# A convolution's last sums moved between engines, a weight slot passed over one group later, and loads that wait

## The chip, the cores and the metric

One core of one Trainium2 chip runs the whole program. The metric is the device time of one execution in microseconds (us), as the median over runs. The engines are TensorE (PE), VectorE (DVE), ScalarE (ACT), GpSimd (POOL) and SyncE (SP, which here issues transfers only).

## The reference, cut to what matters

Two layers over 256 tokens of width 2048, all in float32. Layer 0 mixes tokens by a convolution module, layer 1 by latent attention; each is followed by a SwiGLU block with a hidden width of 5632.

```python
def conv_module(h, w_pw1, b_pw1, w_dw, b_dw, ln_g, ln_b, w_pw2, b_pw2):
    a, gate = jnp.split(h @ w_pw1 + b_pw1, 2, axis=-1)
    v = a * jax.nn.sigmoid(gate)
    v = depthwise causal convolution of v over the tokens, 31 taps per channel, + b_dw
    v = jax.nn.silu(layernorm(v, ln_g, ln_b))
    return v @ w_pw2 + b_pw2

h = h + conv_module(rmsnorm(h), ...)                    # layer 0; layer 1: h + mla(rmsnorm(h), ...)
h = h + (silu(r @ w_gate) * (r @ w_up)) @ w_down        # r = rmsnorm(h), in both layers
```

## The kernel before, in words

**Split weights.** A float32 product is made as three faster products of "high" and "low" parts. So each weight group (1 MB, 128 x 2048 numbers, usually 4 blocks of 128 rows by 512 columns) is loaded into a slot of `raw`; ScalarE copies it, rounded, to `w_hi` (`hi`, `f_hi`), then VectorE writes the rest `raw - w_hi` to `w_lo` (`lo`, `f_lo`), and TensorE multiplies. `raw`, `w_hi` and `w_lo` have four slots each. SyncE waits until the low part of a slot's last group is made before it loads the next group there; ScalarE waits until TensorE has used the slot of `w_hi` and `w_lo`.

**The convolution.** The first product (`w_pw1`) is made in eight halves, s = 0 to 7, each of two tiles (mm = 0, 1) of 128 channels by 256 tokens, from four groups j = 0 to 3. For j = 2 and 3 the low part is not made by VectorE: ScalarE writes the negative high part to `w_lo`, and GpSimd issues a transfer that adds `raw` to it (`conv_low`, semaphore `lo_added`). After TensorE has the tiles, ScalarE makes the sigmoid of the gate (`gate_sigmoid`), VectorE multiplies (`gated`), and the 31 taps are shared out. For s < 7 ScalarE makes 10 products of a tap with the shifted tile into slots of `row_bc`, GpSimd adds them up for both tiles at once (128 x 512, `conv_sums`), and VectorE does the other 21 taps in PSUM (`tap`, a multiply-add each) and adds GpSimd's sum to them. In the last half TensorE does 12 of the taps with diagonal matrices (`conv_rows_last`, which ends with a product for the finished sums, after the wait for `conv_step`); ScalarE does 5 and VectorE 14. Then come the statistics of the layer norm (`row_stats`), the norm, the transposes and the second product (`w_pw2`, groups from G_PW2 on). In the last half TensorE makes tile 0 first (`last_tile0`). ScalarE copies the high part of the first `w_pw2` group between the two tiles.

**The SwiGLU block** (`ffn(l)`, l = 0, 1) goes through the hidden width in 11 chunks of 512, c = 0 to 10. For c >= 1 the parts of one chunk run in the order Q1, R1, Q3, Q5, D0, R2, D1, Q6, D2, Q7, Q2 and so on; Q, R, G and U are groups of the gate and up weights (the Q and R ones form block products by Strassen's method), D0 to D3 are groups of the down weights that use the hidden values of chunk c - 1. TensorE's own order is Q1, R1, Q3, the transposes of chunk c - 1 (`hidden`), Q5, D0, R2, D1, Q6, D2. After the transposes ScalarE writes `a_hi` and VectorE `a_lo`, both in their functions `hidden(c - 1)`; D0 needs both. R2's weights are sums of others: VectorE's `t1_lo_and_t2` and `t2_lo_and_t4` and ScalarE's `t1_hi` and `t2_hi` make them in turn. The slot of a group in `w_hi` and `w_lo` goes round by position (`f_w`); since 182 groups in a layer are not a multiple of four, two slots are passed over, in the chunks 3 and 6 (`F_SKIPS`), at D0. Each engine has one queue in program order, written out by hand in the four blocks.

Of the kernel before, what the change touches and what calls it, by code (L numbers as in the profile page):

```python
# [36 lines left out]
S = 256  # L37
# [7 lines left out]
RING = 4  # L45
# [9 lines left out]
DIAG_PART = 2 * PE_TAPS_LAST // (HALVES - 2)  # L55

PROD_TAPS = (10,) * (HALVES - 1) + (5,)
PROD_TAP = [sum(PROD_TAPS[:s]) for s in range(HALVES + 1)]
PROD_ADD = [sum(PROD_TAPS[:s]) - s for s in range(HALVES + 1)]
# [83 lines left out]
def f_w(q):  # L143


    return (q + sum(q >= f_pos(c, D0) for c in F_SKIPS)) % RING
# [28 lines left out]
def prod_tap0(s):  # L175
    return PE_TAPS_LAST if s == HALVES - 1 else 0


def dve_tap0(s):
    return prod_tap0(s) + PROD_TAPS[s]  # L180

DVE_STEP = [1 + 2 * sum(TAPS - dve_tap0(r) + 1 for r in range(s)) for s in range(HALVES + 1)]
# [23 lines left out]
def encoder(nc, x, positions, attn_norm_g, ffn_norm_g, final_norm_g, conv_w_pw1, conv_b_pw1, conv_w_dw,  # L208
# [3 lines left out]
    with ctx:  # L212
# [279 lines left out]

        def norm_counts(n):

            return KT * n
# [18 lines left out]
        def _(sp):  # L514
# [40 lines left out]
            def square_loads(w, g0):  # L555
                for j in range(KG):
                    load(tile_rows(w, slice(GK * j, GK * j + GK), slice(0, CH)), g0 + j)
                with sp.Fori(0, CC - 1) as i:
                    for j in range(KG):
                        load(tile_rows(w, slice(GK * j, GK * j + GK), bass.ds(i * CH + CH, CH)), g0 + KG + j, i, KG)  # L560
            for n in range(CC):
# [3 lines left out]
            def ffn_loads(l):  # L565
                wg, wu, wd = ffn_w_gate[l], ffn_w_up[l], ffn_w_down[l]

                def f_load(q, src):
# [5 lines left out]
                    elif l == 0:  # L574
                        sp.wait_ge(out_added, TT)
                        sp.wait_ge(prod_added, PROD_ADD[HALVES])
# [80 lines left out]
        def _(pool):  # L657
# [15 lines left out]
            def conv_sums(s):  # L673
# [3 lines left out]
                for n in range(1, PROD_TAPS[s]):  # L677
                    pool.wait_ge(prod_done, 2 * (PROD_TAP[s] + n) + 2 if s < HALVES - 1 else
                                 2 * PROD_TAP[s] + PROD_TAPS[s] + n + 1)
# [5 lines left out]
            for s in range(HALVES):  # L685
# [3 lines left out]
                conv_sums(s)  # L689
# [14 lines left out]
            pool.wait_ge(prod_added, PROD_ADD[HALVES])  # L704
# [26 lines left out]
        def _(act):  # L731
# [75 lines left out]
            def product_of(s, n, mm):  # L807

                m, tile, w = 2 * (s % 2) + mm, 2 * s + mm, prod_tap0(s) + n
                if n == 0 and s >= 2:  # L810
                    act.wait_ge(conv_tr, TT * (s - 1))
                elif n > 0 and PROD_ADD[s] + n > PROD_SLOTS:
# [4 lines left out]
                dst = acc[:, m, :] if n == 0 else prod_slot(s, n)[:, S * mm:S * mm + S]  # L817
# [32 lines left out]
            for mm in range(2):  # L850
                gate_sigmoid(HALVES - 1, mm)
                for n in range(PROD_TAPS[HALVES - 1]):
                    product_of(HALVES - 1, n, mm)
# [55 lines left out]
            def ffn(l):  # L909
# [87 lines left out]
                for c in range(1, FC):  # L997
                    parts_hi(c, D0)
                    t1_hi(c)
                    q1_out(c)  # L1000
                    hidden(c - 1)
                    t2_hi(c)
# [140 lines left out]
        def _(dve):  # L1143
# [109 lines left out]
            def conv_half(s):  # L1253
# [3 lines left out]
                w0 = dve_tap0(s)  # L1257
                steps = TAPS - w0
# [9 lines left out]
                def tap(w, mm):  # L1268
                    m, tile = 2 * u + mm, 2 * s + mm
                    if w == w0:  # L1270
# [5 lines left out]
                    dve.wait_ge(conv_step, DVE_STEP[s] + (steps * mm + w - w0 if last else 2 * (w - w0) + mm - 1))  # L1276
                    dve.scalar_tensor_tensor(bank[mm], vbuf[:, m, w:w + S], tap_col[:, w, tile:tile + 1],
                                             bank[mm], ALU.mult, ALU.add).then_inc(conv_step, 1)

                if last:  # L1280
                    for mm in range(2):
                        gated(mm)
                        for w in range(w0, TAPS):
                            tap(w, mm)
                else:
                    gated(0)
                    gated(1)
                    lo(G_PW1 + KG * (s + 1) + 1)
                    for w in range(w0, TAPS):
                        tap(w, 0)  # L1290
                        tap(w, 1)
                    if s < HALVES - 2:
                        lo(G_PW1 + KG * (s + 2))
                for mm in range(2):
                    m = 2 * u + mm
                    dve.wait_ge(prod_added, PROD_ADD[s + 1])
                    dve.wait_ge(conv_step, DVE_STEP[s] + (steps * (mm + 1) if last else 2 * steps + mm - 1))
                    dve.tensor_tensor(acc[:, m, :], acc[:, m, :], bank[mm], ALU.add).then_inc(conv_step, 1)
# [140 lines left out]
            def ffn(l):  # L1439
# [137 lines left out]
                for c in range(1, FC):  # L1577
                    parts_lo(c, D0)
                    t1_lo_and_t2(c)
                    hidden(c - 1)  # L1580
# [748 lines left out]
```

## Time and profile before

| | us |
|---|---|
| median of 3 runs (2004.69 to 2005.74) | 2005.21 |
| the profiled execution: its own time | 2006.77 |
| the profiled execution: span from first to last instruction | 2004.9 |
| PE busy | 1957.0 |
| DVE busy | 1623.5 |
| ACT busy | 1144.8 |
| POOL busy | 223.3 |

The span is what the trace covers; the 1.9 us between it and the execution's own time lie outside of the records. Matmuls are pipelined, so two that follow each other overlap in the records: what counts is the distance from start to start.

### The profile page before, as it was taken

To read this page: it belongs to the slowest core of one execution; us is meant where nothing else is said; L and a number is where in the kernel's file an instruction comes from. 1 tells how busy PE (TensorE), PEld (TensorE's weight loads), DVE (VectorE), ACT (ScalarE), POOL (GpSimd) and SP (SyncE) were. 2 spreads that over 40 slices of the span, in tenths; PEclk is the share of its full clock that TensorE was granted. 3 is DMA by queue.
4 is the path that set the end of the run, shared out by engine and by line. 5 is a ranking of instruction groups with operands and counts; after the bars stand their busy time and mean duration, and the time that the engine had idled before them with its cause. 6 is when DMAs were issued, how large, how long until landed. Compare 5 with 4: busy or idle time off the path is not lost.

```text
span 2004.9 us, 25061 instructions
## 1 busy us (share of the span) xinstructions
PE 1957.0 (98%) x9934; PEld 1669.9 (83%) x9934; DVE 1623.5 (81%) x1782; ACT 1144.8 (57%) x1140; POOL 223.3 (11%) x187
## 2 busy tenths in 40 slices
PE   8999799999999999999999999999999999999998
PEld 7999788888788888888888998887888888888886
DVE  7999896888888888888876774588888888888885
ACT  5888644555555555555544654356555555655553
POOL 0555200010010100100010000000110000100002
PEclk9999899999999999999999999999999999999999
DMA  8999364899999989999845435559989999999983
GB/s 277 254 254 259 114 213 152 235 266 276 237 227 258 263 273 244 226 264 253 249 155 141 136 135 177 191 176 276 242 225 256 262 278 232 231 257 264 279 210 126
DMA packets 253830, 453.37 MB, mean 226 GB/s; under 512 B 18708, under 2 KB 60444, under 8 KB 251420
## 3 DMA queue, kind: packets, MB, share of 16 engines
q1 hardware_dynamic: 207968, 349.73, 50.3%
q0 software_dynamic: 44256, 98.57, 28.6%
q10 hardware_dynamic: 1500, 3.61, 0.5%
q8 instruction: 72, 1.18, 0.2%
q14 instruction: 34, 0.28, 0.0%
HBM read 435.10 MB, written 2.10 MB: 218 GB/s over the span
## 4 chain that ended last, share of the span: by engine, by line
PE 81%; DMA 9%; DVE 6%; ACT 2%; issue 2%; SPq 0%; POOL 0%; ACTq 0%; DVEq 0%; POOLq 0%
PE ps L1769 77%; DMA raw<-in_conv_w_pw_dram 4%; DMA w_lo<-raw 3%; DVE w_lo L1159 2%; DMA raw<-in_ffn_w_up_dram 1%; PE ps L2010 1%; ACT w_lo L751 1%; ACT w_hi L896 1%; PE ps L2264 0%; PE ps L2265 0%; PE ps L2245 0%; DMA resid<-in_x_dram 0%; DVE raw L1527 0%; DVE w_lo L1525 0%; DVE x_lo L1186 0%
## 5 line engine op out<-in xcount | busy, mean ns | idle before, releaser
L1159 DVE TENSOR_TENSOR w_lo<-raw,w_hi 128x2048 fp32r<-128x2048 f32 x224 | 510.2, 2291 | 148.6 <-ACT w_hi L896 148.6
L896 ACT ACTIVATE w_hi<-raw 128x2048 fp32r<-128x2048 f32 x224 | 426.9, 1916 | 347.4 <-PE ps L1769 215.6
L1769 PE MATMUL ps<-w_hi,x_hi 128*128 128x512 f32 x1168 | 455.7, 390 | 2.2 <-DVE x_lo L1344 1.4
L1769 PE MATMUL ps<-w_hi,x_lo 128*128 128x512 f32 x1168 | 454.5, 389 | 0.0
L1769 PE MATMUL ps<-w_lo,x_hi 128*128 128x512 f32 x1168 | 454.4, 389 | 0.0
L1769 PE MATMUL ps<-w_hi,a_hi 128*128 128x512 f32 (+1 forms) x768 | 292.9, 381 | 7.4 <-DVE a_lo L1444 7.4
L1769 PE MATMUL ps<-w_hi,a_lo 128*128 128x512 f32 (+1 forms) x768 | 292.1, 380 | 0.0
L1769 PE MATMUL ps<-w_lo,a_hi 128*128 128x512 f32 (+1 forms) x768 | 292.0, 380 | 0.0
L1769 PEld LDWEIGHTS ps<-w_hi,x_hi 128*128 128x128 f32 x1168 | 219.3, 188 | 49.1 <-DVE x_lo L1186 1.4
L1769 PEld LDWEIGHTS ps<-w_hi,x_lo 128*128 128x128 f32 x1168 | 219.2, 188 | 45.8
L1769 PEld LDWEIGHTS ps<-w_lo,x_hi 128*128 128x128 f32 x1168 | 219.3, 188 | 45.2
L746 ACT ACTIVATE w_hi<-raw 128x2048 fp32r<-128x2048 f32 x88 | 167.0, 1913 | 94.3 <-PE ps L1769 69.8
L696 POOL DMA_DIRECT2D raw<-in_ffn_w_up_dram x60 | 77.1, 1285 | 1245.2 <-DVE w_lo L1159 1245.2
L1154 DVE TENSOR_TENSOR w_lo<-raw,w_hi 128x2048 fp32r<-128x2048 f32 x74 | 169.0, 2290 | 41.0 <-ACT w_hi L746 40.7
L1769 PEld LDWEIGHTS ps<-w_hi,a_hi 128*128 128x128 f32 x768 | 144.4, 188 | 36.8 <-issue 9.7
L1769 PEld LDWEIGHTS ps<-w_hi,a_lo 128*128 128x128 f32 x768 | 144.5, 188 | 27.6
L1769 PEld LDWEIGHTS ps<-w_lo,a_hi 128*128 128x128 f32 x768 | 144.5, 188 | 27.1
L1159 DVE TENSOR_TENSOR w_lo<-row_bc,w_hi 128x2048 fp32r<-128x2048 f32 x60 | 137.4, 2290 | 31.8 <-ACT w_hi L896 31.7
L1769 PE MATMUL ps<-x_hi,w_hi 128*128 128x256 f32 (+1 forms) x512 | 147.4, 288 | 11.0 <-DMA w_lo<-raw 11.0
L896 ACT ACTIVATE w_hi<-row_bc 128x2048 fp32r<-128x2048 f32 x60 | 114.6, 1911 | 58.1 <-PE ps L1769 58.1
L1769 PE MATMUL ps<-x_lo,w_hi 128*128 128x256 f32 (+1 forms) x512 | 145.7, 284 | 0.0
L1769 PE MATMUL ps<-x_hi,w_lo 128*128 128x256 f32 (+1 forms) x512 | 145.7, 284 | 0.0
(241 smaller groups left out, 2996.0 us busy)
## 6 DMA issues: line engine op xcount, KB each, us to landing
raw<-in_ffn_w_down_dram SPq DMA_DIRECT2D x66, 1024.0 KB, 8.1
raw<-in_ffn_w_up_dram POOLq DMA_DIRECT2D x60, 1024.0 KB, 8.8
raw<-in_ffn_w_gate_dram SPq DMA_DIRECT2D x50, 1024.0 KB, 6.3
raw<-in_ffn_w_up_dram SPq DMA_DIRECT2D x48, 1024.0 KB, 5.9
row_bc<-in_ffn_w_gate_dram SPq DMA_DIRECT2D x38, 1024.0 KB, 5.6
raw<-in_conv_w_pw_dram SPq DMA_DIRECT2D x64, 512.0 KB
row_bc<-in_ffn_w_down_dram SPq DMA_DIRECT2D x22, 1024.0 KB, 5.8
b<-in_ffn_w_up_dram SPq DMA_DIRECT2D x40, 512.0 KB, 5.1
```

The costliest lines, as they stand in the source:

```text
L696: pool.dma_start(f_raw_tile(l, q).rearrange("p (k n) -> p k n", k=GK), w_of(l, p, c), accum_op=ALU.add).then_inc(f_added[f_raw(q)], 16)
L746: act.activation(w_hi[:, slot, :], raw[:, slot, :], ACT.Copy).then_inc(hi_done, 1)
L751: act.activation(w_lo[:, slot, :], raw[:, slot, :], ACT.Copy, scale=-1.0).then_inc(neg_done, 1)
L896: act.activation(f_w_tile(w_hi, l, q), f_raw_tile(l, q), ACT.Copy).then_inc(f_hi_done, 1)
L1154: dve.tensor_tensor(w_lo[:, g % RING, :], raw[:, g % RING, :], hi32(w_hi[:, g % RING, :]), ALU.subtract).then_inc(lo_dve, 1)
L1159: dve.tensor_tensor(f_w_tile(w_lo, l, q), f_raw_tile(l, q), hi32(f_w_tile(w_hi, l, q)), ALU.subtract).then_inc(f_lo_done, 1)
L1769: ins = pe.matmul(dst, lhsT, rhs, start=first and n == 0, stop=last and n == len(pairs) - 1, skip_group_check=skip)
L2010: ins = pe.transpose(ps[:, hidden_bank(c) + b, S * kk + P * t:S * kk + P * t + P], ff_h[:, t, P * m:P * m + P], ident[:, :])
```

## The change

The last half of the convolution is shared out anew: ScalarE makes 8 products for tile 0 and 7 for tile 1 (5 and 5 before), VectorE does 11 and 12 taps (14 and 14), TensorE 12 as before. GpSimd adds these products up tile by tile, in instructions of 128 x 256 (7 and 6; before 4 of 128 x 512 for both), from eight small slots, and VectorE adds GpSimd's sum to its own right behind the taps of each tile. SyncE waits for GpSimd's two adding transfers of the last half before it loads the first `w_pw2` groups. The slot passed over in the chunks 3 and 6 is passed over at D1, not at D0. In chunk 1 `a_lo` is made ahead of the sums for R2, on VectorE and on ScalarE.

```diff
 DIAG_PART = 2 * PE_TAPS_LAST // (HALVES - 2)
-PROD_TAPS = (10,) * (HALVES - 1) + (5,)
-PROD_TAP = [sum(PROD_TAPS[:s]) for s in range(HALVES + 1)]
-PROD_ADD = [sum(PROD_TAPS[:s]) - s for s in range(HALVES + 1)]
+PROD_LAST = (8, 7)
+PROD_TAPS = (10,) * (HALVES - 1)
+PROD_TAP = [sum(PROD_TAPS[:s]) for s in range(HALVES)]
+PROD_ADD = [sum(PROD_TAPS[:s]) - s for s in range(HALVES)]
+PROD_ADD_LAST = [PROD_ADD[HALVES - 1] + sum(PROD_LAST[:mm]) - mm for mm in range(3)]
+PROD_END = PROD_ADD_LAST[2]
 PROD_SLOTS = 4
...
-    return (q + sum(q >= f_pos(c, D0) for c in F_SKIPS)) % RING
+    return (q + sum(q >= f_pos(c, D1) for c in F_SKIPS)) % RING
...
-def prod_tap0(s):
+def prod_tap0(s, mm):
     return PE_TAPS_LAST if s == HALVES - 1 else 0
-def dve_tap0(s):
-    return prod_tap0(s) + PROD_TAPS[s]
-DVE_STEP = [1 + 2 * sum(TAPS - dve_tap0(r) + 1 for r in range(s)) for s in range(HALVES + 1)]
+def prod_taps(s, mm):
+    return PROD_TAPS[s] if s < HALVES - 1 else PROD_LAST[mm]
+def dve_tap0(s, mm):
+    return prod_tap0(s, mm) + prod_taps(s, mm)
+DVE_STEP = [1 + sum(TAPS - dve_tap0(r, mm) + 1 for r in range(s) for mm in range(2)) for s in range(HALVES + 1)]
...
+        def prod_slot_last(mm, n):
+            i = PROD_ADD_LAST[mm] + n - 1
+            return row_bc[:, S * (i % (2 * PROD_SLOTS)):S * (i % (2 * PROD_SLOTS)) + S]
         def norm_counts(n):
...
                         load(tile_rows(w, slice(GK * j, GK * j + GK), bass.ds(i * CH + CH, CH)), g0 + KG + j, i, KG)
+            for j in range(ADDED_FROM, KG):
+                wait_lo(sp, G_PW1 + KG * (HALVES - 1) + j)
             for n in range(CC):
...
                         sp.wait_ge(out_added, TT)
-                        sp.wait_ge(prod_added, PROD_ADD[HALVES])
+                        sp.wait_ge(prod_added, PROD_END)
                     sp.dma_start(f_raw_tile(l, q).rearrange("p (k n) -> p k n", k=GK), src).then_inc(f_in[f_raw(q)], 16)
...
                 for n in range(1, PROD_TAPS[s]):
-                    pool.wait_ge(prod_done, 2 * (PROD_TAP[s] + n) + 2 if s < HALVES - 1 else
-                                 2 * PROD_TAP[s] + PROD_TAPS[s] + n + 1)
+                    pool.wait_ge(prod_done, 2 * (PROD_TAP[s] + n) + 2)
                     if s == 0 and n == 1:
...
                         conv_low(G_PW1 + KG * (s + 1) + j)
-                conv_sums(s)
+                    conv_sums(s)
+            def conv_sums_last(mm):
+                one = acc[:, 2 * ((HALVES - 1) % 2) + mm, :]
+                for n in range(1, PROD_LAST[mm]):
+                    pool.wait_ge(prod_done, 2 * PROD_TAP[HALVES - 1] + sum(PROD_LAST[:mm]) + n + 1)
+                    pool.wait_ge(prod_added, PROD_ADD_LAST[mm] + n - 1)
+                    pool.tensor_tensor(one, one, prod_slot_last(mm, n), ALU.add).then_inc(prod_added, 1)
+            for mm in range(2):
+                conv_sums_last(mm)
...
             pool.wait_ge(rstd_ready, RSTD[3])
-            pool.wait_ge(prod_added, PROD_ADD[HALVES])
+            pool.wait_ge(prod_added, PROD_END)
             half = ROPE // 2
...
-                m, tile, w = 2 * (s % 2) + mm, 2 * s + mm, prod_tap0(s) + n
+                m, tile, w = 2 * (s % 2) + mm, 2 * s + mm, prod_tap0(s, mm) + n
                 if n == 0 and s >= 2:
                     act.wait_ge(conv_tr, TT * (s - 1))
+                elif n > 0 and s == HALVES - 1:
+                    act.wait_ge(prod_added, max(PROD_ADD_LAST[0], PROD_ADD_LAST[mm] + n - 2 * PROD_SLOTS))
                 elif n > 0 and PROD_ADD[s] + n > PROD_SLOTS:
...
                 act.wait_ge(glu_done, tile + 1)
-                dst = acc[:, m, :] if n == 0 else prod_slot(s, n)[:, S * mm:S * mm + S]
+                if n == 0:
+                    dst = acc[:, m, :]
+                elif s < HALVES - 1:
+                    dst = prod_slot(s, n)[:, S * mm:S * mm + S]
+                else:
+                    dst = prod_slot_last(mm, n)
                 act.activation(dst, vbuf[:, m, w:w + S], ACT.Copy, scale=tap_col[:, w, tile:tile + 1]
...
                 gate_sigmoid(HALVES - 1, mm)
-                for n in range(PROD_TAPS[HALVES - 1]):
+                for n in range(PROD_LAST[mm]):
                     product_of(HALVES - 1, n, mm)
...
                     parts_hi(c, D0)
-                    t1_hi(c)
+                    if c > 1:
+                        t1_hi(c)
                     q1_out(c)
                     hidden(c - 1)
+                    if c == 1:
+                        t1_hi(c)
                     t2_hi(c)
...
                 last = s == HALVES - 1
-                w0 = dve_tap0(s)
-                steps = TAPS - w0
+                w0 = [dve_tap0(s, mm) for mm in range(2)]
+                steps = TAPS - w0[0]
                 bank = [ps[:, 6 + u, S * mm:S * mm + S] for mm in range(2)]
...
                     m, tile = 2 * u + mm, 2 * s + mm
-                    if w == w0:
+                    if w == w0[mm]:
                         dve.wait_ge(glu_done, tile + 1)
...
                         return
-                    dve.wait_ge(conv_step, DVE_STEP[s] + (steps * mm + w - w0 if last else 2 * (w - w0) + mm - 1))
+                    dve.wait_ge(conv_step, DVE_STEP[s] + ((steps + 1) * mm + w - w0[mm] if last else 2 * (w - w0[mm]) + mm - 1))
                     dve.scalar_tensor_tensor(bank[mm], vbuf[:, m, w:w + S], tap_col[:, w, tile:tile + 1],
                                              bank[mm], ALU.mult, ALU.add).then_inc(conv_step, 1)
+                def with_products(mm, added, step):
+                    m = 2 * u + mm
+                    dve.wait_ge(prod_added, added)
+                    dve.wait_ge(conv_step, DVE_STEP[s] + step)
+                    dve.tensor_tensor(acc[:, m, :], acc[:, m, :], bank[mm], ALU.add).then_inc(conv_step, 1)
...
                         gated(mm)
-                        for w in range(w0, TAPS):
+                        for w in range(w0[mm], TAPS):
                             tap(w, mm)
-                else:
-                    gated(0)
-                    gated(1)
-                    lo(G_PW1 + KG * (s + 1) + 1)
-                    for w in range(w0, TAPS):
-                        tap(w, 0)
-                        tap(w, 1)
-                    if s < HALVES - 2:
-                        lo(G_PW1 + KG * (s + 2))
+                        with_products(mm, PROD_ADD_LAST[mm + 1], (steps + 1) * mm + TAPS - w0[mm])
+                    row_stats(s - 1)
+                    return
+                gated(0)
+                gated(1)
+                lo(G_PW1 + KG * (s + 1) + 1)
+                for w in range(w0[0], TAPS):
+                    tap(w, 0)
+                    tap(w, 1)
+                if s < HALVES - 2:
+                    lo(G_PW1 + KG * (s + 2))
                 for mm in range(2):
-                    m = 2 * u + mm
-                    dve.wait_ge(prod_added, PROD_ADD[s + 1])
-                    dve.wait_ge(conv_step, DVE_STEP[s] + (steps * (mm + 1) if last else 2 * steps + mm - 1))
-                    dve.tensor_tensor(acc[:, m, :], acc[:, m, :], bank[mm], ALU.add).then_inc(conv_step, 1)
+                    with_products(mm, PROD_ADD[s + 1], 2 * steps + mm - 1)
                 if s > 0:
...
                     parts_lo(c, D0)
+                    if c == 1:
+                        hidden(c - 1)
                     t1_lo_and_t2(c)
-                    hidden(c - 1)
+                    if c > 1:
+                        hidden(c - 1)
                     t2_lo_and_t4(c)
```

## Rows read from the trace of the kernel before

**Rows 1.** The page: busy us, share of the span and instructions of each engine.

```profile
PE 1957.0 (98%) x9934; PEld 1669.9 (83%) x9934; DVE 1623.5 (81%) x1782; ACT 1144.8 (57%) x1140; POOL 223.3 (11%) x187
```

**Rows 2.** Waits of PE, whole span: what, for whom, us in total, times, longest.

```profile
PE ps L1769 <- DMA w_lo<-raw: 11.0, 7, 4.1
PE ps L1769 <- DVE a_lo L1444: 7.4, 6, 1.6
PE ps L1800 <- DVE ytmp L1328: 4.8, 1, 4.8
```

**Rows 3.** Windows: length; busy us (x instructions) per engine; PEclk, DMA share, GB/s.

```profile
206.00:210.00 4.00, 0.00 (x0) 0.00 (x0) 4.00 (x12) 0.82 (x3) 3.57 (x4) 0.74 0.95 292
210.00:214.00 4.00, 3.98 (x18) 3.99 (x19) 2.98 (x9) 0.00 (x0) 0.37 (x1) 0.50 0.79 272
```

**Rows 4.** Timeline of PE, end of the convolution: start, us, engine, line [idle before <-releaser].

```profile
210.02 0.58 PE L1769 MATMUL ps<-x_hi,w_hi 128*128 128x256 f32 x1 [4.12 <-DMA w_lo<-raw]
...
221.25 10.88 PE L1769 MATMUL ps<-diag_last,scratch 128*128 128x128 f32 x96
...
232.17 1.16 PE L1769 MATMUL ps<-ident,scratch 128*128 128x128 f32 x8
```

**Rows 5.** Timeline of VectorE, the same stretch.

```profile
212.23 0.75 DVE L1311 BATCH_NORM_STATS2 bn<-ytmp 128x6 f32<-128x256 f32 x2
...
215.77 0.48 DVE L1264 SCALAR_TENSOR_TENSOR scratch<-ps,bias_col,scratch 128x256 f32<-128x256 f32 x1 [2.79 <-ACT scratch L804]
...
216.87 6.79 DVE L1277 SCALAR_TENSOR_TENSOR ps<-scratch,tap_col,ps 128x256 f32<-128x256 f32 x13
...
224.67 6.79 DVE L1277 SCALAR_TENSOR_TENSOR ps<-scratch,tap_col,ps 128x256 f32<-128x256 f32 x13
```

**Rows 6.** Timeline of ScalarE, the last half's products and a weight copy.

```profile
216.77 1.70 ACT L818 ACTIVATE row_bc<-scratch,tap_col 128x256 f32<-128x256 f32 x4
...
218.37 1.90 ACT L746 ACTIVATE w_hi<-raw 128x2048 fp32r<-128x2048 f32 x1
```

**Rows 7.** Timeline of GpSimd, the last adding transfer and the last sums.

```profile
196.28 0.86 POOL L671 DMA_DIRECT2D w_lo<-raw  x1 [3.49 <-ACT w_lo L751]
...
225.13 5.56 POOL L684 TENSOR_TENSOR scratch<-scratch,row_bc 128x512 f32<-128x512 f32 x4 [14.76 <-ACT row_bc L818]
```

**Rows 8.** DMA queues from 185 to 262: packets, MB, share of 16 engines.

```profile
q0 software_dynamic: 288, 2.10, 13.6%
```

**Rows 9.** Groups of GpSimd by form: busy us, mean ns.

```profile
L716 POOL MEMSET ytmp<- 128x384 f32 x1 | 0.4, 411 | 0.0
...
L663 POOL MEMSET scratch<- 128x128 f32 x1 | 0.2, 205 | 0.1
```

**Rows 10.** Timeline of PE, the SwiGLU chunks 1 and 3 of layer 0.

```profile
393.46 0.47 PE L1769 MATMUL ps<-w_hi,a_hi 128*128 128x512 f32 x1 [0.95 <-DVE a_lo L1444]
...
519.39 0.47 PE L1769 MATMUL ps<-w_hi,a_hi 128*128 128x512 f32 x1 [1.43 <-DVE a_lo L1444]
```

**Rows 11.** Timeline of VectorE, chunk 1 of layer 0.

```profile
390.23 1.22 DVE L1525 TENSOR_TENSOR w_lo<-raw,w_hi 128x1024 fp32r<-128x1024 f32 x1
391.49 1.23 DVE L1527 TENSOR_TENSOR raw<-raw,b 128x1024 f32<-128x1024 f32 x1
392.63 1.28 DVE L1444 TENSOR_TENSOR a_lo<-ps,a_hi 128x512 fp32r<-128x512 f32 x2
```

**Rows 12.** Timeline of ScalarE, chunk 1 of layer 0.

```profile
387.50 1.04 ACT L956 ACTIVATE w_hi<-raw 128x1024 fp32r<-128x1024 f32 x1
```

**Rows 13.** Timeline of ScalarE, chunk 3 of layer 0.

```profile
512.01 1.92 ACT L896 ACTIVATE w_hi<-raw 128x2048 fp32r<-128x2048 f32 x1 [2.91 <-PE ps L1769]
...
525.22 1.92 ACT L896 ACTIVATE w_hi<-raw 128x2048 fp32r<-128x2048 f32 x1 [1.87 <-PE ps L1769]
...
527.88 0.60 ACT L975 ACTIVATE scratch<-ps 128x512 f32<-128x512 f32 x1 [0.74 <-PE ps L1769]
```

**Rows 14.** Timeline of VectorE, chunk 3 of layer 0.

```profile
513.96 2.29 DVE L1159 TENSOR_TENSOR w_lo<-raw,w_hi 128x2048 fp32r<-128x2048 f32 x1 [2.53 <-ACT w_hi L896]
```

## The prediction

> **What bounds the kernel now.** I read the page first: TensorE is busy 1957.0 of 2004.9 us, 98% [rows 1], so only its waits and stretches at a lower clock can be gained. The waits of PE come next [rows 2]. Three causes bear on this change: 11.0 us for GpSimd's adding transfers into `w_lo`, the longest 4.1; 7.4 us in six waits for `a_lo`, none over 1.6; and 4.8 us for the layer norm, at the end of the convolution. So there are two places, and each is read from its timelines.
>
> **The end of the convolution, before.** TensorE stands 4.12 us until 210.02, for the last adding transfer [rows 4], which GpSimd issued at 196.28 [rows 7]: 13.7 us in flight. Then it runs at half clock: 0.74 granted from 206 to 210, 0.50 (1.2 of 2.4 GHz) from 210 to 214 [rows 3]. So tile 0 of the last half and its sigmoid are late, and VectorE, done with the half before at 212.23 + 0.75 = 212.98, stands 2.79 us until 215.77 [rows 5]. From there VectorE sets the end: gate and 14 taps take from 215.77 to 216.87 + 6.79 = 223.66, the same again for tile 1, and its two additions end where TensorE's last product starts, 232.17 [rows 4]. TensorE's diagonal products end with it (221.25 + 10.88 = 232.13), so both must come earlier.
>
> **The held loads.** Before, three `w_pw2` loads of 1 MB could run beside the two adding transfers: two as soon as their slots were free, one after the first adding transfer. After, all four start behind the second. The two adding transfers together are 2.10 MB and 13.6% of sixteen engines over 77 us, 10.5 us of all the engines, so 5.2 us each if alone [rows 8]. The first is issued 4.4 us before the second, so the second should land near 196.28 + 0.86 + 1.0 (what is left of the first) + 5.2 = 203.4. TensorE asks for it at 210.02 - 4.12 = 205.9. The bounds are 203.4 and the old 209.97; I take the lower, since the row of the queue measures these very transfers. The wait and the half clock go. A tile of 24 matmuls takes under 3 us at full clock, so tile 0 is there by 209, and what is late next is VectorE, at 212.98. This part gains 2.8 us and no more, and would still give that if the transfer landed at 209 without a drop of the clock.
>
> What queues behind the new waits is SP's whole stream: the four loads, 4 MB, go out near 203.4. At the 272 to 292 GB/s of [rows 3] the first lands before 210, the last near 219. ScalarE copies the first between the two tiles, at about 217 (below), the others after 224. That is cover of some 7 and 5 us, so I cost the hold at nothing.
>
> **The taps.** A tap is 6.79 / 13 = 0.52 us [rows 5]. Tile 0 loses three, so gate and taps take 7.89 - 1.57 = 6.3 us: 212.98 to 219.3. Meanwhile ScalarE makes 8 products at 1.70 / 4 = 0.42 us; the second one, which GpSimd needs to begin, is done 1.0 us after the gate (before 216.25, and the second at 217.2) [rows 5, 6], so at 214.5. GpSimd then has 7 additions of 128 x 256. The trace has none of that size. The nearest row is the same addition at 128 x 512: 5.56 / 4 = 1.39 us with its hand-over [rows 7]. The ends are 0.70 (all of it goes by width) and 1.39 (none does). A memset of GpSimd takes 205 ns at 128 columns and 411 at 384 [rows 9], so 0.10 is fixed; with that and about 0.12 of hand-over I take 0.82. Seven are 5.7 us: GpSimd ends at 220.3, a full 1.0 us after VectorE's taps. VectorE waits, since the sum is now behind each tile's taps and the gate of tile 1 stands behind it. With 0.5 for the addition it goes on at 220.8. The copy of the first `w_pw2` group, 1.9 us [rows 6], ends near 219, and the second sigmoid follows it before 220, so it is hidden. Tile 1 takes 7.89 - 1.04 = 6.85 us, to 227.7; GpSimd's 6 additions end at 221.3 + 1.0 + 4.9 = 227.2 and are covered by 0.5 us. With 0.5 more the sums are ready at 228.2, against 232.17. **Gain 4.0 us.** TensorE has its last 96 diagonal products done before: half of them after the second gate, 221.3 + 5.4 = 226.7. All that follows, the 4.8 us wait for the norm too, moves with it unchanged.
>
> The Trainium skill (GPSIMD Engine Reference, 3.1) gives about 2.6 cycles per element at 1.2 GHz for a two-input addition, so by my estimate from it 256 columns less save 0.55 us of the 1.39, an addition takes 0.84, and the end of the convolution would come 0.1 us later than in my sum; no run here shows that size.
>
> A rule that speaks against the change: GpSimd now works beside the taps for some 10.7 us instead of 5.6. If taps went at half speed beside it, the 5 us more would cost about 2.5. But 13 taps take 6.79 us with no addition beside them (216.87) and 6.79 with four (224.67) [rows 5, 7], so I cost it at nothing. The Trainium skill (GPSIMD Engine Reference, 8) says that GpSimd shares its SBUF interfaces with VectorE, in contention with VectorE instructions that have two SBUF inputs. By it these taps, whose second tensor lies in PSUM, are spared, and the rows agree.
>
> **The slot.** A group whose slot follows the one passed over waits for TensorE to use the third group before it, not the fourth. At D0 that is R1: in chunk 3 ScalarE copies D0 only at 512.01, after 2.91 us of waiting for TensorE [rows 13]. VectorE then stands 2.53 us and starts D0's low part at 513.96 [rows 14]; the sums for R2 (2.4 us) and `a_lo` follow, and TensorE is 1.43 us late at 519.39 [rows 10]. With the slot passed over at D1, D0 needs Q1, long used, so VectorE goes on behind Q5 and `a_lo` comes up to 2.5 us earlier: the wait goes. The third group back is now what D1, Q6 and D2 wait for: Q5, D0 and R2. Priced from D0's start T, now 517.96: D0 is used at T + 5.8 (before 525.22), R2 at T + 8.4 (before 527.88) [rows 10, 13]. D1 is ready by then, and ends at T + 14. Q6 is copied at T + 5.8, takes 1.9 and 2.3, and is ready at T + 10; needed at T + 14. D2's copy starts at T + 8.4 and ends at 10.3; its low part waits for Q6's and for two additions of the first down block (1.3), so it ends at T + 13.5, needed at T + 16.7. The cover is 4 and 3 us. Chunks 3 and 6 of two layers are four places.
>
> **Chunk 1.** D0's low part ends at 390.3; the R2 sums (390.23, 391.49) stand ahead of `a_lo` (392.63), which TensorE awaits 0.95 us, until 393.46 [rows 10, 11]. Moved ahead, `a_lo` comes 2.4 us earlier and the wait goes; in layer 1 the same wait is the 1.6 of [rows 2]. The price is R2: from 390.3, `a_lo` 1.2, low part 1.2, sum 1.2, ScalarE's copy 1.0 [rows 12], low part 1.2, with hand-overs 396.3. TensorE needs it after D0, 392.5 + 5.8 = 398.3: 2 us of cover. D1, behind it on both engines, comes at about 399.8 and is needed at 398.3 + 2.6 = 400.9, with one us of cover; that is the thinnest.
>
> So all six waits go: **gain 7.4 us** [rows 2]. If cover runs out, the lateness of R2 or D1 takes their place.
>
> **The sum.** 4.0 + 7.4 = 11.4 us, from 2006.77 (span 2004.9, 1.9 outside) to 1995.4 by the profiled execution. That one is 1.56 above the median of the runs; the steps don't depend on that, so I subtract from the median: 2005.21 - 11.4 = 1993.8.
>
> **Rivals.** One: an addition of GpSimd costs 1.39 whatever its width. Then tile 0 goes on at 214.5 + 9.7 + 0.5 = 224.7, and the sums are ready at 225.2 + 1.0 + 8.3 + 0.5 = 235.0, 2.9 later than before: 2005.21 + 2.9 - 7.4 = 2000.7. For it: no row shows the size; against it the memsets. Chance 0.08.
>
> Two: the adding transfer is slow by itself and not by the loads beside it, and lands at 209.97 again. The 2.8 us stay: 1996.6. For it: 10.5 us of service for two, but 13.7 in flight for one. Chance 0.10.
>
> Three: half of the SwiGLU waits come back at R2, D1 or D2, since VectorE and ScalarE run in fixed order with little cover: 2005.21 - 4.0 - 3.7 = 1997.5. For it the one us at D1; against it that TensorE waits in no other chunk. Chance 0.14.
>
> Four, slower: in chunks 3 and 6 Q6's copy, held until D0 is used, blocks ScalarE's queue (D2, the copy-out of Q5, Q7, Q2), and D2's low part comes too late. It decides from 3.2 us of lateness. If it reaches 6.5, TensorE stands 3.3 us in four places and runs at half clock after, which at 206 to 214 cost about 2 us [rows 3]: 1993.8 + 4 x 5.3 = 2015. Chance 0.04.
>
> The forecast has the other 0.64, and between 1992.5 and 1995.5 by GpSimd's 0.70 to 0.90. The range is 1991.5 to 1999.5. What a measurement can tell from no change is 0.2%, 4 us: faster 0.92, same 0.04, slower 0.04.
>
> **What would show it.** The profile after: no wait of PE for `w_lo` at the last half and a clock near 1.00 from 206 to 214; the last adding transfer under 9 us in flight; VectorE's gate of tile 0 at about 213, its wait for GpSimd about 1 us, 13 additions of 0.6 to 0.8; the last products near 228; no PE row for `a_lo`. The prediction is wrong if a new PE wait for `w_lo` of R2, D1, Q6 or D2 appears, if ScalarE waits for the first `w_pw2` group, or if the 11 us are not in these two places.

## The result and the profile after

The changed kernel takes 1991.89 us (median of 6 runs, 1991.35 to 1993.32), the kernel before 2005.18 in the same comparison: a ratio of 0.9935, 95% interval 0.9923 to 0.9948, so 13.3 us less with an interval of some 10 to 15. The forecast was 11.4 less (1993.8). The profiled execution of the changed kernel took 1993.20, its span is 1991.4; before they were 2006.77 and 2004.9, so the profiles differ by 13.5 us of span. In a later comparison the changed kernel, unaltered, took 1994.62 against 2004.12 (0.9953, 0.9941 to 0.9965). Both intervals hold the forecast ratio of 0.9943.

The waits of PE over the whole span, in the form of [rows 2]: no row for `a_lo` is left, the six waits for adding transfers all end by 184.38 (none is at the last half), and VectorE's `scratch` rows are new.

```profile
PE ps L1812 <- DMA w_lo<-raw: 6.2, 6, 3.0
PE ps L1843 <- DVE ytmp L1368: 4.8, 1, 4.8
...
PE ps L1812 <- DVE scratch L1319: 1.3, 1, 1.3
...
PE ps L1812 <- DVE scratch L1298: 0.8, 1, 0.8
```

The clock in the windows of [rows 3]: 1.00 in both, 0.74 and 0.50 before.

```profile
206.00:210.00 4.00, 4.00 (x36) 4.00 (x35) 4.00 (x12) 0.47 (x1) 3.25 (x3) 1.00 1.03 395
210.00:214.00 4.00, 4.00 (x36) 4.00 (x35) 3.89 (x10) 1.42 (x4) 0.44 (x1) 1.00 1.05 389
```

The timelines of VectorE and then of PE for the last half, as in [rows 4, 5]. The column in brackets is the time for which the engine stood, and for whom.

```profile
211.35 0.75 DVE L1351 BATCH_NORM_STATS2 bn<-ytmp 128x6 f32<-128x256 f32 x2
212.01 0.47 DVE L1298 SCALAR_TENSOR_TENSOR scratch<-ps,bias_col,scratch 128x256 f32<-128x256 f32 x1
...
213.10 5.21 DVE L1311 SCALAR_TENSOR_TENSOR ps<-scratch,tap_col,ps 128x256 f32<-128x256 f32 x10
219.56 0.42 DVE L1319 TENSOR_TENSOR scratch<-scratch,ps 128x256 f32<-128x256 f32 x1 [1.25 <-POOL scratch L711]
...
221.00 5.74 DVE L1311 SCALAR_TENSOR_TENSOR ps<-scratch,tap_col,ps 128x256 f32<-128x256 f32 x11
226.84 0.42 DVE L1319 TENSOR_TENSOR scratch<-scratch,ps 128x256 f32<-128x256 f32 x1
```

```profile
214.14 5.52 PE L1812 MATMUL ps<-diag_last,scratch 128*128 128x128 f32 x48
220.43 5.62 PE L1812 MATMUL ps<-diag_last,scratch 128*128 128x128 f32 x48 [0.77 <-DVE scratch L1298]
227.31 1.16 PE L1812 MATMUL ps<-ident,scratch 128*128 128x128 f32 x8 [1.25 <-DVE scratch L1319]
233.27 6.18 PE L1843 MATMUL ps<-ident,ytmp 128*128 128x128 f32 x32 [4.80 <-DVE ytmp L1368]
```

The reader is to see that VectorE goes from its statistics of the half before (211.35 + 0.75) straight to the gate (212.01): the 2.79 us of [rows 5] are gone. Then it stands 1.25 us for GpSimd, and TensorE stands for VectorE: 0.77 us before the diagonal products of tile 1 and 1.25 before the last products. TensorE, whose diagonal products ended with the sums before, now has room.

GpSimd's transfer and its additions, as in [rows 7]; the line after them is GpSimd's group of the same additions, with their mean:

```profile
195.36 0.86 POOL L686 DMA_DIRECT2D w_lo<-raw  x1 [3.46 <-ACT w_lo L775]
...
213.56 5.97 POOL L711 TENSOR_TENSOR scratch<-scratch,row_bc 128x256 f32<-128x256 f32 x7 [4.02 <-ACT row_bc L849]
221.46 5.09 POOL L711 TENSOR_TENSOR scratch<-scratch,row_bc 128x256 f32<-128x256 f32 x6 [1.93 <-ACT row_bc L849]
```

```profile
L711 POOL TENSOR_TENSOR scratch<-scratch,row_bc 128x256 f32<-128x256 f32 x13 | 9.5, 729 | 7.5 <-ACT row_bc L849 6.0
```

In the SwiGLU block of layer 0, VectorE in chunk 1, with `a_lo` (L1484) ahead of the sums, as in [rows 11], and ScalarE in chunk 3, as in [rows 13]:

```profile
380.51 4.50 DVE L1193 TENSOR_TENSOR w_lo<-raw,w_hi 128x2048 fp32r<-128x2048 f32 x2 [2.36 <-ACT w_hi L927]
385.12 1.29 DVE L1484 TENSOR_TENSOR a_lo<-ps,a_hi 128x512 fp32r<-128x512 f32 x2
...
387.82 1.23 DVE L1567 TENSOR_TENSOR raw<-raw,b 128x1024 f32<-128x1024 f32 x1
```

```profile
501.16 3.72 ACT L927 ACTIVATE w_hi<-raw 128x2048 fp32r<-128x2048 f32 x2 [4.00 <-DMA raw<-in_ffn_w_up_dram]
...
511.98 1.92 ACT L927 ACTIVATE w_hi<-row_bc 128x2048 fp32r<-128x2048 f32 x1 [0.88 <-PE ps L1812]
517.41 1.92 ACT L927 ACTIVATE w_hi<-raw 128x2048 fp32r<-128x2048 f32 x1 [3.52 <-PE ps L1812]
520.13 1.92 ACT L927 ACTIVATE w_hi<-raw 128x2048 fp32r<-128x2048 f32 x1 [0.80 <-PE ps L1812]
```

In chunk 3 the copies of Q5 and D0 now follow each other at once (x2 at 501.16), and the waits for TensorE stand where the prediction put them: before D1's copy (511.98), before Q6's (517.41, 3.52 us), before D2's (520.13). With D0 starting near 511.7, Q6's copy was forecast at 517.5 and D2's at 520.1. TensorE waits for none of them.

**Where the 13.5 us went.** Three pieces, each between two instructions that the change leaves alone:

| piece | before | after | |
|---|---|---|---|
| start to VectorE's statistics of the seventh half | 212.23 | 211.35 | -0.88 |
| from there to TensorE's first transposes of the norm | 25.89 | 21.92 | -3.97 |
| the two pieces with a SwiGLU block each: layer 0 from TensorE's row behind its wait for `x_lo` (335.76 before) to its row behind the first wait for `qr_pad` (1096.46), layer 1 from 1302.02 to the end of the span | 1463.58 | 1454.95 | -8.63 |

(The second piece is 212.23 to 238.12 and 211.35 to 233.27; the third 760.70 + 702.88 and 756.73 + 698.22.) The sum is 13.48. The two stretches between the pieces took 97.6 and 205.6 us in both profiles.

These are differences between one profile and one other, and a piece of the kernel before isn't the same in every execution. Five profiles have no edit in the second piece (before, and four of the experiments below: only the slot, only the order, the slot at R2, the order in every chunk). It took 25.89, 26.24, 26.31, 25.41 and 24.70 us there, mean 25.7. What differs is how long VectorE stands for the late tile 0: 2.79, 3.15, 3.21, 2.32 and 1.61 us. Without this stand the five are 23.09 to 23.10. Three profiles have no edit in the SwiGLU blocks (before, only the held loads, only the split): 1463.58, 1461.56 and 1462.53, mean 1462.6. The profile before is the longest of the three.

### The profile page after: what moved, and what is told of

The parts are those of the page before. It is cut to its first block, busy times and chain, and to the rows that moved or that the text cites. A ratio compares the mean times of both kernels' runs of the same rounds, so it can differ in the third digit from the quotient of the medians.

```text
span 1991.4 us, 25085 instructions
## 1 busy us (share of the span) xinstructions
PE 1953.9 (98%) x9934; PEld 1668.7 (84%) x9934; DVE 1619.2 (81%) x1777; ACT 1145.6 (58%) x1145; POOL 227.6 (11%) x196
## 4 chain that ended last, share of the span: by engine, by line
PE 86%; DMA 7%; DVE 3%; ACT 2%; issue 1%; SPq 0%; POOL 0%; ACTq 0%; DVEq 0%; POOLq 0%
PE ps L1812 83%; DMA raw<-in_conv_w_pw_dram 4%; DMA w_lo<-raw 3%; DVE ps L1311 1%; PE ps L2053 1%; ACT w_lo L775 1%; PE ps L2307 0%; PE ps L2308 0%; PE ps L2288 0%; DMA resid<-in_x_dram 0%; DVE w_lo L1188 0%; SPq L560 0%; PE ps L1862 0%; POOL scratch L711 0%; PE ps L1851 0%
```

## The experiments

Each is an edit of the kernel before, unless it says otherwise. The times of single runs scattered by several us, so each is read by its ratio to the runs of before beside it (in brackets its 95% interval) and, for the causes, by the pieces of the table above. These leave out the scatter of the first piece, but not their own, given there. "Less than before" is said of the profile before.

**Only the held loads.**

```diff
+            for j in range(ADDED_FROM, KG):
+                wait_lo(sp, G_PW1 + KG * (HALVES - 1) + j)
             for n in range(CC):
```

> Only the held loads, on the kernel before. My theory (hold and split are one knot: VectorE's queue and TensorE's diagonal products both end at 232.13 before, so each edit frees only one of them): the last adding transfer lands near 204, VectorE starts the last half without its 2.8 us of standing, TensorE's diagonal products come 6 us earlier. Gain 2.8 us, 2002.4. The additive rival: half of the 4 us at the convolution's end, 2.0 us, 2003.2. Rival 'the transfer is slow by itself': it stays at 13.7 us in flight, 2005.2.

Measured: 2001.79 us, ratio 0.9984 (0.9973 to 0.9994). VectorE and PE in the last half:

```profile
213.35 0.74 DVE L1313 BATCH_NORM_STATS2 bn<-ytmp 128x6 f32<-128x256 f32 x2
214.02 0.46 DVE L1266 SCALAR_TENSOR_TENSOR scratch<-ps,bias_col,scratch 128x256 f32<-128x256 f32 x1
...
221.80 0.48 DVE L1266 SCALAR_TENSOR_TENSOR scratch<-ps,bias_col,scratch 128x256 f32<-128x256 f32 x1
```

```profile
222.33 5.62 PE L1771 MATMUL ps<-diag_last,scratch 128*128 128x128 f32 x48 [1.67 <-DVE scratch L1266]
230.40 1.16 PE L1771 MATMUL ps<-ident,scratch 128*128 128x128 f32 x8 [2.44 <-DVE scratch L1300]
236.35 5.34 PE L1802 MATMUL ps<-ident,ytmp 128*128 128x128 f32 x32 [4.80 <-DVE ytmp L1330]
```

The last adding transfer is 8.3 us in flight, against 13.7 before. VectorE doesn't stand before the gate (213.35 + 0.74, then 214.02), and TensorE stands for it 1.67 and 2.44 us. The second piece is 236.35 - 213.35 = 23.0 us: 2.9 less than before, and 0.1 less than the 23.1 that the unedited ones take without VectorE's stand. So the held loads take away the whole stand, 2.79 us in the profile before (forecast 2.8) and 1.6 to 3.2 in the others. The rival of a transfer that is slow by itself is ruled out: over all twelve profiles the last adding transfer is 12.8 to 13.9 us in flight in the six whose loads are not held, and 7.2 to 8.4 in the six whose loads are. The additive rival (2.0 us) fits less well.

**Only the new split of the taps.** The changed kernel without the held loads, with the slot at D0 and the old order in chunk 1.

```diff
-PROD_TAPS = (10,) * (HALVES - 1) + (5,)
+PROD_LAST = (8, 7)
+PROD_TAPS = (10,) * (HALVES - 1)
...
+            for mm in range(2):
+                conv_sums_last(mm)
```

> Only the new split of the last half's taps (8 and 7 products, 11 and 12 VectorE taps, GpSimd tile by tile), loads not held. My theory: VectorE's part would end 1.1 us earlier, but TensorE, delayed by the adding transfer, still ends its diagonal products at 232.13 and now sets the end: gain 0 to 0.2 us, 2005.1. The additive rival: the two taps-per-tile and the waits are worth 4.0 - 2.8 = 1.2 us alone, 2004.0.

Measured: 2003.74 us, ratio 0.9992 (0.9982 to 1.0003). PE and VectorE:

```profile
208.37 0.58 PE L1804 MATMUL ps<-x_hi,w_hi 128*128 128x256 f32 x1 [3.79 <-DMA w_lo<-raw]
...
219.87 10.88 PE L1804 MATMUL ps<-diag_last,scratch 128*128 128x128 f32 x96
230.59 1.06 PE L1804 MATMUL ps<-ident,scratch 128*128 128x128 f32 x8
236.44 5.90 PE L1835 MATMUL ps<-ident,ytmp 128*128 128x128 f32 x32 [4.79 <-DVE ytmp L1363]
```

```profile
210.72 0.74 DVE L1346 BATCH_NORM_STATS2 bn<-ytmp 128x6 f32<-128x256 f32 x2
214.38 0.48 DVE L1293 SCALAR_TENSOR_TENSOR scratch<-ps,bias_col,scratch 128x256 f32<-128x256 f32 x1 [2.92 <-ACT scratch L826]
...
229.25 0.42 DVE L1314 TENSOR_TENSOR scratch<-scratch,ps 128x256 f32<-128x256 f32 x1
...
231.24 0.88 DVE L1346 BATCH_NORM_STATS2 bn<-ps 128x6 f32<-128x256 f32 x2 [0.90 <-PE ps L1804]
```

The last transfer is 13.6 us in flight, TensorE stands 3.79 us for it, and VectorE stands 2.92 us for tile 0. VectorE has its sums at 229.25 + 0.42 = 229.7, but TensorE's 96 diagonal products run from 219.87 to 230.75, and now VectorE stands 0.90 us for TensorE. The piece is 236.44 - 210.72 = 25.7 us. That alone tells nothing, since the unedited ones scatter from 24.7 to 26.3; without its stand it is 22.8, where theirs are 23.1. So the split alone is worth 0.3 us, close to the forecast (0 to 0.2), and not the 1.2 of the additive rival. With the loads held it is worth 23.0 - 21.92 = 1.1. The two edits end in one place, and what the split saves on VectorE comes out only when TensorE too is early.

**Only the slot.**

```diff
-    return (q + sum(q >= f_pos(c, D0) for c in F_SKIPS)) % RING
+    return (q + sum(q >= f_pos(c, D1) for c in F_SKIPS)) % RING
```

> Only the slot passed over at D1 instead of D0, on the kernel before. My theory: four waits for a_lo go, 4.81 us by the rows, and each removed wait is worth about 0.2 us more than its row says, since a matmul is recorded longer (0.39) than the distance at which the next one starts (0.23): gain 5.7 us, 1999.5. The rival that the extra of the changed kernel's result comes from somewhere else: 4.8 us, 2000.4. The rival that the waits come back at R2, D1 or D2: 2 to 3 us.

Measured: 1996.67 us, ratio 0.9954 (0.9941 to 0.9968): 9.2 us less, 6.4 to 11.8, where 5.7 was expected. In the profile the four waits of chunks 3 and 6 are gone and nothing came in their place; the two of chunk 1 are there, but only 0.57 and 0.17 us long (0.95 and 1.61 before). The SwiGLU pieces are 757.24 + 698.90 = 1456.14, 7.4 less than before: 4.81 for the rows of the four waits, 1.8 for the shorter waits of chunk 1, which this edit does not touch, and 0.8 for the four rows' overlap (below). The first piece ended at 210.03, 2.2 us earlier than in the profile before, with no edit there either. Whether the other runs of this kernel had as short waits and as early a first piece, no profile shows, so a part of the 9.2 us stays unexplained. The profile does settle the rivals: no wait came back at R2, D1 or D2.

**Only the order in chunk 1.**

```diff
                 for c in range(1, FC):
                     parts_lo(c, D0)
+                    if c == 1:
+                        hidden(c - 1)
                     t1_lo_and_t2(c)
-                    hidden(c - 1)
+                    if c > 1:
+                        hidden(c - 1)
```

(and on ScalarE as in the change.)

> Only a_lo ahead of R2's sums in chunk 1, on the kernel before. My theory: two waits of 0.95 and 1.61 go, with 0.2 more each: gain 3.0 us, 2002.2. Rival, that the cover of one us at D1 runs out: a wait of PE for w_lo appears in chunk 1 and the gain is 1 to 2 us.

Measured: 2002.34 us, ratio 0.9990 (0.9980 to 0.9999). Both waits of chunk 1 are gone, no row of PE for `w_lo` appears in the SwiGLU blocks, and one wait for `a_lo` of 0.18 us turned up in chunk 9 of layer 0. The SwiGLU pieces are 1460.82, 2.8 less than before (forecast 3.0), and 1.8 less than the mean of the three unedited. The thin cover of D1 held.

**The slot one group earlier, at R2.**

```diff
-    return (q + sum(q >= f_pos(c, D0) for c in F_SKIPS)) % RING
+    return (q + sum(q >= f_pos(c, R2) for c in F_SKIPS)) % RING
```

> The slot passed over at R2 in the chunks 3 and 6, on the kernel before (one group past D0, one short of D1). My theory: it matters who stands ahead of a_lo in VectorE's queue. R2's sums do, and their first copy on ScalarE now waits for TensorE to use Q3, until 514.2 on the scale of the profile before. Then the sums and a_lo end about 0.6 us earlier than before, and waits for a_lo of about 0.75 us stay in each of the four places, out of 1.1 to 1.4: gain 1.8 us or a little more. Rival: any place other than D0 frees D0, and all four waits go, 5.7 us.

Measured: 2002.93 us, ratio 0.9990 (0.9979 to 1.0001). PE in the chunks 3 and 6 of layer 0; layer 1 has 0.81 and 0.79:

```profile
516.72 0.47 PE L1769 MATMUL ps<-w_hi,a_hi 128*128 128x512 f32 x1 [0.78 <-DVE a_lo L1444]
...
704.25 0.47 PE L1769 MATMUL ps<-w_hi,a_hi 128*128 128x512 f32 x1 [0.81 <-DVE a_lo L1444]
```

The SwiGLU pieces are 1461.56, 2.0 less than before. The rows of the four places are 1.6 less, and those of chunk 1, which this edit does not touch, 0.9 (1.68 in sum here, 2.56 before). Four waits of 0.78 to 0.81 us are left where 0.75 was expected, so the rival that any place other than D0 frees all four is ruled out. VectorE in chunk 3:

```profile
507.18 4.49 DVE L1159 TENSOR_TENSOR w_lo<-raw,w_hi 128x2048 fp32r<-128x2048 f32 x2 [2.26 <-ACT w_hi L896]
513.49 1.23 DVE L1525 TENSOR_TENSOR w_lo<-raw,w_hi 128x1024 fp32r<-128x1024 f32 x1 [1.82 <-ACT w_hi L956]
...
515.89 1.28 DVE L1444 TENSOR_TENSOR a_lo<-ps,a_hi 128x512 fp32r<-128x512 f32 x2
```

D0 itself was free here as at D1: its low part follows Q5's at once (x2 at 507.18). But R2's sums stand ahead of `a_lo`, and before the first of them VectorE stands 1.82 us for ScalarE's copy (L956), which waited for Q3.

**`a_lo` ahead of the sums in every chunk,** the slot still at D0.

```diff
                 for c in range(1, FC):
                     parts_lo(c, D0)
-                    t1_lo_and_t2(c)
                     hidden(c - 1)
+                    t1_lo_and_t2(c)
```

(and on ScalarE `t1_hi` behind `hidden`, in every chunk.)

> a_lo ahead of R2's sums in every chunk, on the kernel before, the slot still passed over at D0. My theory: the sums (2.4 us) are more than each wait (at most 1.6), so all six waits go, also those of the chunks 3 and 6, and R2 keeps some 2 us of cover in the ordinary chunks: gain 8.6 us, of it all in the SwiGLU blocks. Rival: R2 or D1 comes late in the 18 chunks in which nothing waited before, and PE rows for w_lo appear there; each 0.3 us of them would cost 5 us.

Measured: 1995.94 us, ratio 0.9959 (0.9946 to 0.9971). No wait for `a_lo` and none for `w_lo` in the SwiGLU blocks; their pieces are 756.35 + 698.18 = 1454.53, 9.1 less than before (8.1 less than the mean of the three; forecast 8.6) and as short as in the changed kernel (1454.95). So the new place of the slot is not the only cure: this order alone takes all six waits away, in these profiles.

**Seven and seven products,** in the changed kernel.

```diff
-PROD_LAST = (8, 7)
+PROD_LAST = (7, 7)
```

> The changed kernel with 7 and 7 products in the last half, 12 and 12 VectorE taps. In the changed kernel VectorE waits 1.25 us for GpSimd's seventh addition (0.85 us each) after tile 0. With six, GpSimd ends near 218.7 and VectorE, with one tap more (0.52), near 218.9: the wait goes, and the end of the convolution comes 0.6 us earlier than in the changed kernel. Rival, that TensorE's diagonal products bind: nothing.

Measured: 1992.81 us, ratio to before 0.9936 (0.9914 to 0.9958). VectorE's wait for GpSimd is gone; the second piece is 235.24 - 213.94 = 21.3 us, 0.6 less than the changed kernel's 21.92, as expected. (With the loads held and 12 taps on TensorE, VectorE stands for no late tile, and the changed kernel's piece came out at 21.92 twice, so a difference of 0.6 counts here.) The time doesn't show it, since the first piece ended at 213.94 in this profile.

**Thirteen taps on TensorE,** in the changed kernel, with 7 products and 11 VectorE taps for each tile.

```diff
-PE_TAPS_LAST = 12
-DIAG_PART = 2 * PE_TAPS_LAST // (HALVES - 2)
-PROD_LAST = (8, 7)
+PE_TAPS_LAST = 13
+DIAG_PART = -(-2 * PE_TAPS_LAST // (HALVES - 2))
+PROD_LAST = (7, 7)
```

> As before it, but TensorE takes 13 taps of the last half, ScalarE 7 and VectorE 11 of each tile. TensorE's part grows by 0.46 us per tile, from 5.5 to 6.0; it waits for VectorE 0.77 and 1.25 us in the changed kernel, so there is room: TensorE ends near 226.1 and VectorE near 226.2 on the scale of the changed kernel's profile, where the last products start at 227.3. Gain over the changed kernel 1.0 us, 0.4 more than with 7 and 7. Rival: two more diagonals on ScalarE (0.3 us each) slow the earlier halves, or TensorE binds: no gain over 7 and 7.

Measured: 1991.13 us, ratio to before 0.9934 (0.9914 to 0.9954).

```profile
212.78 11.78 PE L1812 MATMUL ps<-diag_last,scratch 128*128 128x128 f32 x104
224.88 1.16 PE L1812 MATMUL ps<-ident,scratch 128*128 128x128 f32 x8 [0.32 <-DVE scratch L1319]
230.83 5.69 PE L1843 MATMUL ps<-ident,ytmp 128*128 128x128 f32 x32 [4.79 <-DVE ytmp L1368]
```

The second piece is 230.83 - 210.04 = 20.8 us, 1.1 less than in the changed kernel. TensorE's 104 diagonal products run without a gap, and it stands only 0.32 us for the sums. The forecast for the piece was 1.0. Whether the two more diagonals cost the earlier halves anything doesn't show in their scatter.

**The changed kernel again,** unaltered, and the thirteen taps with `a_lo` ahead in every chunk:

```diff
-                    if c == 1:
-                        hidden(c - 1)
+                    hidden(c - 1)
                     t1_lo_and_t2(c)
-                    if c > 1:
-                        hidden(c - 1)
```

> The changed kernel unaltered, for a second profile and times beside the next kernel. Theory: the piece from VectorE's statistics of the seventh half to TensorE's first transposes of the norm is again 21.9 us (25.9 before), and the two SwiGLU pieces of the profile together again about 1455 us (1463.6 before), each within 0.3; what differs between two profiles of one kernel is the eight halves ahead, whose end has scattered from 210.0 to 213.9 us in the profiles so far with no edit there. If a part of the gain came from those halves, their end would be near 211.4 again and the median near 1991.9.

> 13 taps on TensorE, 7 products and 11 VectorE taps in both tiles of the last half, and a_lo ahead of R2's sums in every chunk, not only in chunk 1; all else as in the changed kernel. Theory: the piece at the convolution's end is 20.8 us again, the SwiGLU pieces stay at 1454.5 to 1455, since no wait for a_lo is left to gain there: 1.1 us less than the changed kernel, 1990.8. Rival: with the slot at D1 and the sums later, R2 or D1 comes late and PE rows for w_lo appear in the SwiGLU blocks.

Measured: 1994.62 us (0.9953, 0.9941 to 0.9965) and 1992.92 us (0.9948, 0.9935 to 0.9961). For the changed kernel the second piece is 235.33 - 213.41 = 21.92 us again, to the hundredth; the SwiGLU pieces are 1455.45, with one wait of 0.25 us in chunk 9; but the first piece ends at 213.41, not 211.35. For the other kernel the second piece is 20.82 and the SwiGLU pieces are 1454.53. By the pieces it is the best version, 1.1 us and some tenths below the changed kernel; by the times 1.7 us below it, with intervals that overlap.

## Why the prediction was right, step by step

The forecast of 11.4 us was right in sign, place and mechanism, and every wait that it said would go is gone. That its size came out near is in part luck, as the last points show. Its terms:

- **The held loads.** The last adding transfer: forecast landing 7.1 us after its issue, measured 8.4 in flight (13.7 before). The clock stayed at 1.00. The gate of tile 0 followed VectorE's own queue at once. Alone 2.9 us against the profile before (forecast 2.8), which is VectorE's stand there; in other profiles that stand is 1.6 to 3.2.
- **The price of the hold.** None: ScalarE waits for none of the four held groups in the profile after, and the stretch from the transposes to layer 0's SwiGLU block is as long as before (97.6 us); its copy of the first group ran at 215.8, and SP issued the first load at 203.8.
- **The taps.** Forecast 25.9 - 4.0; measured 21.92, so 3.97 less. GpSimd's addition is 729 ns by itself and 0.85 with hand-over (5.97 for 7); I had taken 0.82. VectorE's wait for it is 1.25 us (forecast 1.0). The rival of 1.39 whatever the width is ruled out. The estimate of 0.84 from the per-element rate in the Trainium skill (GPSIMD Engine Reference, 3.1) was as near, and this trace agrees with it.
- **The shared interface.** 10 taps take 5.21 us beside GpSimd's additions, 0.52 each, as before. By the Trainium skill (GPSIMD Engine Reference, 8) GpSimd contends with VectorE instructions that have two SBUF inputs or run in a 2-port mode. The trace agrees for these taps, which have one tensor in PSUM. No low part (`raw - w_hi`, two SBUF inputs) ran beside an addition of GpSimd. Four ran beside small operations of GpSimd, from 1035 to 1045 us of the profile after: one took 2.28 us and three 2.32, where the other 70 took 2.28 to 2.30. So what contention this kernel shows is 0.03 us of 2.3.
- **Slot and order.** Forecast 7.4 us, measured 8.6 against the profile before. For that profile this is the term that was sized too small. A wait's row says 1.43 us, but TensorE's starts before it are 1.81 apart (517.58 and 519.39) where 0.23 is the usual distance, and the next start follows 0.31 later: 1.66 lost. A matmul's record is 0.39 long and overlaps the next one, and the row counts the idle time only from the end of the record.

Here are PE's rows around that wait in the profile before:

```profile
517.36 0.39 PE L1769 MATMUL ps<-w_lo,s_hi 128*128 128x512 f32 x1
517.58 0.39 PE L1769 MATMUL ps<-w_hi,s_lo 128*128 128x512 f32 x1
...
519.70 0.40 PE L1769 MATMUL ps<-w_lo,a_hi 128*128 128x512 f32 x1
519.94 0.40 PE L1769 MATMUL ps<-w_hi,a_lo 128*128 128x512 f32 x1
```

All six waits lose 0.23 us more than their rows say. Six times 0.23 and the 7.37 of the rows are 8.75; the pieces show 8.63. The other profiles agree within 0.4: with only the split the pieces are 1462.53, 7.58 over the changed kernel's, for six rows of 6.31 (7.69 with 0.23 each); with the slot at R2, 6.61 for six rows of 4.87 (6.25).

- **The waits of chunk 1.** They were unusually long in the profile that the forecast was read from. In five profiles whose code is the same there they are 0.95, 0.54, 0.96, 0.57 and 0.40 us in layer 0, and 1.61, none, 0.83, 0.17 and 1.28 in layer 1 (before, only the held loads, only the split, only the slot, the slot at R2). They follow the adding transfer of Q5's weights, which GpSimd issues and ScalarE's copy waits for: it was 9.94, 9.53, 9.99, 9.57 and 9.44 us in flight in layer 0, and 10.60, 9.05, 9.83, 9.17 and 10.27 in layer 1. Each of the ten waits is this time less 9.0, to within 0.1. The two waits together are 2.56 us in the profile before and 1.5 on average. So the forecast had 1.1 too much for a typical execution and, with 0.23 left out of each wait, 1.4 too little, and the two errors nearly cancel.
- **The remaining 0.9 us** are the first piece. It ended at 212.23, 211.35, 213.35, 210.72, 210.03, 210.19, 211.25, 211.65, 213.94, 210.04, 213.41 and 211.07 us in the twelve profiles (before, after, then the experiments in the order of this document). Only the two kernels with more diagonals have an edit that TensorE, VectorE or ScalarE reach in it. This is scatter of 3.9 us between executions, and not between chips: 213.35 and 210.03 come from one chip, 213.94 and 210.04 from another. The piece is the stretch in which PE waits for the adding transfers again and again and in which the DMA share is 0.94 to 0.95. The three profiles in which it ended latest had a mean granted clock of 0.98 over its first 190 us, with two stretches of 3.4 us at 0.50 each; the others had 0.99 or 1.00. That is a part of the scatter; what starts it no run shows.

So the 13.3 us of the first comparison and the 9.5 of the second (2004.12 - 1994.62) are the same kernel. By the pieces the change is worth 4.0 + 8.6 = 12.6 us against the profile before. Against the means of the unedited pieces, and with both profiles of the changed kernel (21.92 twice, 1454.95 and 1455.45), it is 3.8 + 7.4 = 11.2 us. That is the better figure for the change itself. It lies as near to the forecast as can be told, and the 1.9 us by which the first comparison exceeds the forecast are not shown to be an effect of the change.

What stays open is why the flight time of these transfers scatters, in layer 1 between 9.05 and 10.60 us: no run held it fixed. Nor was the hold tried with only one of its two waits.

## What to carry to other kernels

Where two engines reach one point together, an edit that speeds up one is worth nothing until the other is early too: 0.3 us alone here, 1.1 with the other edit in. Before moving work between engines, read the end of both. An instruction that must come early belongs ahead in every queue that it passes, and a slot that waits should fall where several microseconds of other work lie before it. A wait of a pipelined TensorE costs a little more than its row says, 0.23 us for each here. A piece of the timeline between two untouched instructions is no exact measure either while a wait for a transfer lies in it: take it from several profiles, or subtract the wait.

## What the runs showed of the hardware that was not expected

Two adding transfers within SBUF, 1 MB each and 4.3 us apart, were 8.1 and 13.7 us in flight beside loads from HBM, and 7.0 and 8.4 us without. The second of them is over 12.7 us in all six profiles with the loads beside it and under 8.5 in all six without. The same 2.10 MB took the same 13.6% of the engines from 185 to 262 in both profiles, so the packets themselves took no longer beside the loads. By this reading the rest of the 13.7 us is time that they queued; no trace shows the queue itself. The four held loads then ran at 389 to 395 GB/s (windows above), against 272 to 292 for loads and adding transfers together [rows 3].
